# Qkv norms and weight splits moved into the first stage, and the sampled tokens' cross attention rebuilt on 32-column quarters with x's reload beside it

## The reference, cut to what matters

```python
(c_q, c_kv, k_r, z_mla, conv_b, conv_c, conv_h, z_conv, q_x, z_x, gates) = split(h @ w_in)
q     = rms_norm(c_q, q_norm_g) @ w_uq          # heads, then rotary on the last 32 columns
c_kv  = rms_norm(c_kv, kv_norm_g);  k_r = rope(k_r)          # both are outputs as well
y_mla = latent_attention(...)                   # prompt: causal; sampled: 4096 cached positions and the new ones
y_x   = softmax(q_x @ mem_k.T * X_SCALE) @ mem_v             # 4 heads of 128, 256 memory rows
m     = sum over branches of sigmoid(gate) * ((y * silu(z)) @ w_p)
h     = layer_norm(alpha * h + m @ w_o)
```

## Time and profile before

| | us |
|---|---|
| median of 3 runs | 1633.55 |
| lowest, highest | 1630.62, 1635.21 |
| the profiled execution, its own time | 1637.49 |
| its span, first to last instruction | 1635.7 |
| PE busy in the span | 1551.4 (95%) |
| DVE, ACT, POOL busy | 679.7, 443.9, 410.4 |
| mean granted TensorE clock | 0.97 |

### The profile page before, as it was taken

The page is one execution under the profiler, slowest core; times in us unless marked ns, Lnnn a source line. Parts: engine busy times, 40 slices in busy tenths (PEclk is TensorE's granted clock), DMA queues, the critical chain, the costliest instruction groups (busy, mean ns, idle before and its releaser), DMA issues.

```text
span 1635.7 us, 26131 instructions
## 1 busy us (share of the span) xinstructions
PE 1551.4 (95%) x10008; PEld 1365.9 (84%) x10008; DVE 679.7 (42%) x1484; ACT 443.9 (27%) x1067; POOL 410.4 (25%) x295
## 2 busy tenths in 40 slices
PE   7996989999999999969699999999999999999997
PEld 7995967775677777744599999999999999999885
DVE  4204457763533333324334435112644347007744
ACT  4212456661554443411211111111111111113200
POOL 3001046672022222000122222222222222124322
PEclk9997989999999999979599999999999999999999
DMA  5200120002634555223611212111111112112321
GB/s 210 76 1 13 31 78 1 1 1 71 196 92 123 159 157 152 69 73 133 174 39 40 52 39 52 46 39 46 41 45 52 46 39 52 39 50 80 117 94 61
DMA packets 101215, 117.88 MB, mean 72 GB/s; under 512 B 11970, under 2 KB 75266, under 8 KB 101092
## 3 DMA queue, kind: packets, MB, share of 16 engines
q1 hardware_dynamic: 99044, 112.02, 23.3%
q0 software_dynamic: 2048, 4.20, 1.0%
HBM read 109.39 MB, written 6.80 MB: 71 GB/s over the span
## 4 chain that ended last, share of the span: by engine, by line
PE 50%; DMA 1%; issue 1%; DVE 0%; POOL 0%; POOLq 0%; SPq 0%; ACT 0%
PE ps L1762 44%; PE ps L1786 5%; DMA p_xs<-x_prompt 1%; PE ps L1736 1%; DMA p_xs<-x_sample 0%; POOL p_h L1858 0%; POOLq L1646 0%; SPq L1676 0%; DVE p_stats L2022 0%; DVE p_h L2033 0%; DVE p_h L2018 0%; DVE p_h L2031 0%; DVE p_xl L1882 0%; ACT p_xh L1797 0%; PE ps L1773 0%
## 5 line engine op out<-in xcount | busy, mean ns | idle before, releaser
L1762 PE MATMUL ps<-p_xh,p_wh 128*128 128x352 f32 (+1 forms) x1152 | 377.1, 327 | 0.9 <-DVE p_xl L1882 0.9
L1762 PE MATMUL ps<-p_xh,p_wl 128*128 128x352 f32 (+1 forms) x1152 | 376.8, 327 | 0.0
L1762 PE MATMUL ps<-p_xl,p_wh 128*128 128x352 f32 (+1 forms) x1152 | 376.5, 327 | 0.0
L1848 POOL TENSOR_TENSOR p_wl<-p_wr,p_wh 128x512 fp32r<-128x512 f32 x120 | 167.1, 1407 | 665.2 <-DVE p_wh L1871 665.2
L1762 PEld LDWEIGHTS ps<-p_xh,p_wh 128*128 128x128 f32 x1152 | 217.0, 188 | 1.0 <-ACT p_xh L1797 1.0
L1762 PEld LDWEIGHTS ps<-p_xl,p_wh 128*128 128x128 f32 x1152 | 217.6, 189 | 0.0
L1762 PEld LDWEIGHTS ps<-p_xh,p_wl 128*128 128x128 f32 x1152 | 216.7, 188 | 0.0
L1871 DVE CAST p_wh<-p_wr 128x512 fp32r<-128x512 f32 x120 | 46.8, 424 | 346.0 <-ACT p_stage L1833 254.4
L1833 ACT ACTIVATE p_stage<-ps 128x384 f32<-128x384 f32 x168 | 79.4, 473 | 366.1 <-PE ps L1762 366.1
L830 POOL TENSOR_SCALAR p_pr<-p_pr,p_rec 128x896 f32<-128x896 f32 (+3 forms) x64 | 109.6, 1722 | 120.1 <-DVE p_rec L792 120.0
L871 POOL DMA_INDIRECT p_rawr<-cache_kr,p_rows x64 | 64.9, 1013 | 223.6 <-PE ps L1159 162.5
(11 more groups left out here) (286 smaller groups left out, 2755.3 us busy)
## 6 DMA issues: line engine op xcount, KB each, us to landing
p_rawc<-cache_ckv SPq DMA_DIRECT2D x256, 128.0 KB
p_wr<-w_in SPq DMA_DIRECT2D x104, 256.0 KB
p_xs<-x_prompt SPq DMA_DIRECT2D x16, 512.0 KB
p_kv<-cache_mem_k SPq DMA_DIRECT2D x8, 512.0 KB, 10.3
p_kv<-cache_mem_v SPq DMA_DIRECT2D x8, 512.0 KB, 10.7
p_wr<-w_o SPq DMA_DIRECT2D x16, 256.0 KB
p_x<-x_prompt SPq DMA_DIRECT2D x8, 512.0 KB, 3.5
y_p<-p_h SPq DMA_DIRECT2D x8, 512.0 KB, 2.6
```

Of the source, the lines that this page charges most:

```text
L1762: last = pe.matmul(ps[:, g % 8, 0:tn], w[:, v % HL, kt % UK, :], x[:, kt, t0:t0 + tn], start=(kt == 0 and q == 0), stop=(kt == nk - 1 and ...
L1848: nc.gpsimd.tensor_tensor(wl[:, v % HL], wr[:, v % RAW], f32(wh[:, v % HL]), ALU.subtract).then_inc(wl_done, 1)
```

## The change: what it does

- **Qkv's preparation.** The roots, all 9 norms, the split of `w_uq`, `w_uk`, `w_uv`, the rotation of k_r, the casts and the loads of tables and norm weights are moved from `make_qkv` to `project_latents`, behind the last latent tile on each engine's list. The split q_x columns get buffers of their own (`whq`, `wlq`), so that the split `w_uq`, `w_uk`, `w_uv` can lie where the latent columns were. `make_qkv` keeps transposes, splits of the transposed tiles, products and the rotation of q; its output DMAs are issued at its start.
- **Cross attention of sampled tokens.** Each head gets its own 32-column quarter of the PE array (`tile_position=(0, h * 32)`): head h's scores go to PSUM rows 32h to 32h+31 (8 rows used, the others zeros), its values to the same rows and 128 columns. Row-wise work is now on 128 partitions; the probabilities are transposed as 128 x 128, the output with one transpose.
- **x's reload in it.** In step r of the same 12-step pipeline PE also transposes x's tile r (`turn_x`), ACT and DVE split it. Keys and x have one pair of PSUM banks each (before: two). The key and value buffers are 6 (before: 8). SP's list is k, v and x tile by tile, each x load from the third on waiting for `turn_x` of two tiles before; then the convolution's loads and the first 4 weight units, which DVE splits in steps 9 to 11 and POOL finishes. `merge` starts at its matmuls. `clear_sems` stands ahead of `cross_decode`; none is between it and `merge`.

```diff
@@ project_latents, DVE behind the loop over the latent tiles
+            dve.wait_ge(squared, 2 * NT)
+            for j, n in ((0, QL), (1, KVL)):
+                last = dve.tensor_scalar(ms[:, :, j:j + 1], k["ssq"][:, :, j:j + 1], 1.0 / n, EPS, ALU.mult, ALU.add)
+            last.then_inc(mean, 1)
...
+            for i in range(NT):
+                r = rows(i)
+                dve.tensor_scalar(tok[0:r, i, 0:QL], tok[0:r, i, 0:QL], rstd[0:r, i, 0:1], None, ALU.mult)
+                dve.scalar_tensor_tensor(out=tok[0:r, i, QL:QL + KVL], in0=tok[0:r, i, QL:QL + KVL],
...
+            for t in range(QT):
+                dve.wait_ge(uq_step, t + 1)
+                dve.tensor_copy(uqh[:, t, :], uq[:, t, :]).then_inc(w_split, 1)
...
@@ project_latents, SP behind its other loads
+            sp.wait_ge(turned, NT)
+            sp.dma_start(gq[:, :], a["q_norm_g"][0].rearrange("(t p) -> p t", p=P),
...
+            sp.wait_ge(wl_done, NW)
+            sp.dma_start(k["cos"][:, :, :], a["cos"]).then_inc(got, 16)
...
@@ project_latents, ACT ahead of the q_x pieces
+            act.wait_ge(mean, 1)
+            nc.scalar.activation(rt[:, :, :], ms[:, :, :], ACT.Sqrt).then_inc(root, 1)
+            act.wait_ge(lat_done, NT)
+            act.wait_ge(k["uq_in"], 48)
+            for j in range(2):
+                nc.scalar.activation(kvh[:, j], k["ukv"][:, j], ACT.Copy).then_inc(kv_split, 1)
...
@@ make_qkv, PE
             def turn(i):
-                pe.wait_ge(normed, i + 1)
...
@@ cross_decode, SP
+            for b in range(DECB):
+                if b >= KVS:
+                    sp.wait_ge(o_done, b - KVS + 1)
+                for j, (name, kv_in) in enumerate((("cache_mem_k", k_in), ("cache_mem_v", v_in))):
+                    sp.dma_start(kv[:, b % KVS, j], a[name][0, b].rearrange("(t p) h d -> p t (h d)", p=P)
+                                 ).then_inc(kv_in[b], 16)
+                x_dma(b)
+            x_dma(NPT)
...
@@ cross_decode, PE
             def turn(b):
-                if b >= 2:
-                    pe.wait_ge(kt_done, b - 1)
+                if b:
+                    pe.wait_ge(kt_done, b)
...
             def scores(b):
                 for h in range(XH):
-                    last = pe.matmul(ps[0:R, 4, 0:MEM], q[:, b, h, :], kT[:, b % 2, h, :], start=(h == 0),
-                                     stop=(h == XH - 1))
+                    last = pe.matmul(ps[h * R:(h + 1) * R, 4, 0:MEM], q[:, b, h, :], kT[:, b % 2, h, :], start=True,
+                                     stop=True, tile_position=(0, h * R))
...
             def values(b):
                 for j in range(MT):
-                    last = pe.matmul(ps[0:R, 6, :], pt[:, b % 2, j, :], kv[:, b, 1, j, :], start=(j == 0),
-                                     stop=(j == MT - 1))
+                    for h in range(XH):
+                        last = pe.matmul(ps[h * R:(h + 1) * R, 6, 0:XD], pt[:, b % 2, j, h * R:(h + 1) * R],
+                                         kv[:, b % KVS, 1, j, h * XD:(h + 1) * XD], start=(j == 0), stop=(j == MT - 1),
+                                         tile_position=(0, h * R))
...
+            def turn_x(i):
+                pe.wait_ge(x_in[i % 2], 16 * (i // 2 + 1))
+                if i:
+                    pe.wait_ge(xh_done, i)
+                    pe.wait_ge(xl_done, i)
+                for t in range(KT):
+                    last = pe.transpose(ps[:, 2 + t // 4, (t % 4) * P:(t % 4) * P + r],
+                                        xs[0:r, i % 2, t * P:(t + 1) * P], k["ident"][0:r, 0:r])
+                last.then_inc(x_turned, 1)
+            for r in range(DECB + 4):
+                in_step(((r, turn), (r - 1, scores), (r - 2, turn_probs), (r - 3, values), (r - 4, turn_out)))
+                if r < NT:
+                    turn_x(r)
+                elif r == NT:
+                    turn_conv()
@@ cross_decode, ACT
+            for r in range(DECB + 2):
+                in_step(((r - 1, exps), (r - 2, keep_probs)))
+                if r < NT:
+                    x_high(r)
@@ cross_decode, DVE
+            for r in range(DECB + 4):
+                in_step(((r, keys), (r - 1, maxima), (r - 3, normalise), (r - 2, inverse), (r - 4, keep_y)))
+                if r < NT:
+                    x_low(r)
+                else:
+                    v = r - NT
+                    dve.wait_ge(w_got[v], 16)
+                    dve.tensor_copy(wh[:, v], wr[:, v]).then_inc(wh_done, 1)
+            dve.wait_ge(w_got[EARLY - 1], 16)
+            dve.tensor_copy(wh[:, EARLY - 1], wr[:, EARLY - 1]).then_inc(wh_done, 1)
@@ cross_decode, POOL
+            for v in range(EARLY):
+                pool.wait_ge(wh_done, v + 1)
+                nc.gpsimd.tensor_tensor(wl[:, v], wr[:, v], f32(wh[:, v]), ALU.subtract).then_inc(wl_done, 1)
@@ hybrid_step
-        cross_decode(nc, ps, a, k, decode_at)
         clear_sems()
-        merge(nc, ps, a, k, keep.at)
+        shared = merge_space(nc, k, keep.at)
+        cross_decode(nc, ps, a, k, keep.at, shared)
+        merge(nc, ps, a, k, shared)
```

More of the change, by code:

```diff
@@ L396, in _ @@
         def _(act):
-            act.wait_ge(mean, 1)
-            nc.scalar.activation(rt[:, :, :], ms[:, :, :], ACT.Sqrt).then_inc(root, 1)
-            act.wait_ge(k["uq_in"], 48)
-            for j in range(2):
-                nc.scalar.activation(kvh[:, j], kv[:, j], ACT.Copy).then_inc(kv_split, 1)
             def hi(i):
@@ L1416, in _, with merge_jobs @@
                 gather_rotary(nc, a, e, n)
-def cross_decode(nc, ps, a, k, at):
-    m = Map(nc, at)
+def merge_jobs():
+    jobs = []
+    for br, z0 in ((1, C_ZC), (2, C_ZX), (0, C_ZM)):
+        for j in range(4):
+            if br == 1:
+                jobs += [("c", br, j, C_C + j * P), ("h", br, j, C_H + j * P), ("b", br, j, C_B + j * P)]
+            jobs.append(("z", br, j, z0 + j * P))
+        gates = [("gate", br, d, C_G + br * D + d * P) for d in range(KT)]
+        projs = [("proj", br, d, d * P) for d in range(KT)]
+        jobs += gates + projs if br == 0 else [job for pair in zip(gates, projs) for job in pair]
+    return jobs
@@ L1594, in merge, with _ @@
-def merge(nc, ps, a, k, at):
+                if r < NT:
[6 more added lines that the diff above has]
+            dve.tensor_copy(wh[:, EARLY - 1], wr[:, EARLY - 1]).then_inc(wh_done, 1)
+        @block.gpsimd
+        def _(pool):
+            for v in range(EARLY):
+                pool.wait_ge(wh_done, v + 1)
+                nc.gpsimd.tensor_tensor(wl[:, v], wr[:, v], f32(wh[:, v]), ALU.subtract).then_inc(wl_done, 1)
@@ L1597, in merge @@
+def merge(nc, ps, a, k, e):
     jobs = merge_jobs()
-    UK = 4
-    units = [(j, u) for j, job in enumerate(jobs) for u in range(1 if job[0] == "proj" else 2)]
+    units = merge_units(jobs)
     first_unit = [next(v for v, (j, _) in enumerate(units) if j == n) for n in range(len(jobs))]
-    RAW, HL, ST = 4, 6, 8
-    m = Map(nc, at)
-    xh, xl = m("p7_xh", [P, KT, T], F32R), m("p7_xl", [P, KT, T], F32R)
-    mt_at = m.at
-    mt = m("p7_mt", [P, KT, T])
-    u_at = m.at
-    uh, ul = m("p7_uh", [P, 4, T], F32R), m("p7_ul", [P, 4, T], F32R)
@@ L1843, in _ @@
         def _(pool):
-            for v in range(NU):
+            for v in range(EARLY, NU):
                 pool.wait_ge(wh_done, v + 1)
```

385 lines of the change are left out of this document (177 added, 208 removed).

## The result

| | before | after |
|---|---|---|
| median, us (4 runs each, same chip) | 1633.61 | 1586.63 |
| lowest, highest | 1630.62, 1635.21 | 1585.85, 1589.11 |
| the profiled execution, its own time | 1637.49 | 1586.74 |
| its span | 1635.7 | 1584.9 |
| mean granted TensorE clock | 0.97 | 0.984 |

The ratio is 0.9725, with a 95% interval of 0.9707 to 0.9743: 47 us faster. The forecast was 1587.0. The sum inside it was right to some 2 us in each of its large terms, and one loss of 2.5 us that it had not foreseen went against them. The new kernel's four times are 1585.85 to 1589.11 us, so that single executions differ by some 3 us and only the trace can tell terms of that size apart.

The account below looks back on a forecast made before the run. PE's gapless 714.06 us of merge matmuls stays untouched, so gains come ahead of it: 14.5 + 1.3 + 30.8 = 46.6 us, against the median 1633.55 giving 1587.0 us; own range 1581 to 1592 (70%), wider range 1579 to 1603.

Parts of the forecast that it names:

- Qkv's preparation: Start of make_qkv: with preparation moved behind the latents, the first product starts at 136.95 instead of 151.44, gaining 14.5 us.
- The cover: DVE's 47.65 us of idle time behind the latents hides the moved work, put at 28 us, leaving 20.
- rival 5: First stage: moved preparation, ACT's root and casts, holds up the q_x pieces; 15.8 us not won, time 1603; chance 3%.
- The clock: First product step in make_qkv: up to 2.5 us more if the clock does not fall; the middle, 1.3 us, taken.
- The stretch: First load of memory keys to first merge matmul, 726.29 to 811.79: the merge starts at 781.0, gaining 30.8 us.
- the ring of 4.62: New cross attention stage: x_low, keys, maxima, exp, probabilities' copy, x_high and hand-overs on DVE and ACT set each step.
- PE's own work per step: New cross attention stage: transposes, scores and values sum to 3.9 us, under the step's 4.6, so PE waits each step.
- Scores and values: Cross attention on quarters of the PE array: scores take 0.55 us and values 0.9 us per step.
- rival 1: New cross attention stage: quarters do not overlap, PE's step is 6.15 us, +10.9 us, time 1598; chance 10%.
- rival 2: New cross attention stage: clock stays at 1.2 GHz, PE's step 7.3 us, 17 us more, time 1604; chance 9%.
- rival 3: New cross attention stage: loads at 174 GB/s bound the step at 9.0 us, +31 us, time 1618; chance 6%.
- Rival 4: Merge: moved buffers slow the 4320 matmuls, slower than before from 6.5% on; at 8% time 1644; chance 2%.

Follow-up runs that it names:

- the kernel with three small changes: Changed kernel with maxima ahead of key copies, x's halves at a multiple of 64 bytes, two of four weight units split in the stage: 1572.81 us, ratio 0.9667.
- the kernel with maxima first: Changed kernel with DVE taking the maxima of scores(r-1) ahead of its copy of keys(r): 1577.07 us, ratio 0.9702.
- the variants of before: Kernel before with only merge placement moved: `mh` low, `oh` in the middle, 1632.69 us; `mh` low, `oh` high, 1633.38; only `oh`, `ol` high, 1635.26.
- the kernel with the aligned halves: Changed kernel with x's halves starting 32 bytes lower, at a multiple of 64 bytes (159680): 1581.96 us, ratio 0.9741.

## Why the prediction was right

**Qkv's preparation, 14.5 us.** Measured 14.81. From the start of the last q_x copy to the first product it took 3.13 us (133.50 to 136.63) where 3.12 was worked out (133.83 to 136.95); the other 0.3 us are the first stage's, which ended sooner in this execution. The cover that was left, put at 20 us or more, was 27.33. No price of the moved norms reached the path, and rival 5 is out.

**The clock, 1.3 us.** Measured 2.53, the upper end of 0 to 2.5. The rows of before could not have decided it, and even the code does not: the kernel with three small changes has the same first two stages, and there the clock fell in the same window, which this is in that kernel:

```profile
136.00:140.00 4.00, 3.68 (x13) 3.71 (x14) 0.97 (x3) 0.00 (x0) 0.00 (x0) 0.57 0.70 183
```

Its variant with `mt` moved has 0.57 there too, six other kernels with this code have 1.00. In the kernel with three small changes the first step took 7.94 us (136.32 to 144.26) in place of 6.45. So the term differs between executions.

**The stretch, 30.8 us.** Measured 32.94, from three terms counted from the end of y_mla. The first x_low starts after 10.43 us (716.79 - 706.36), predicted 12.41 (738.45 - 726.04): the first three transfers landed sooner than in the row of before, turn_x(0) starting after 7.37 us (713.73 - 706.36) and not 9.36 (735.4 - 726.04). The eight steps took 34.21 (751.00 - 716.79), predicted 35.05: the ring of 4.62 was 4.51. From the last x_low to the first merge matmul 8.17, predicted 7.5: DVE's split of a unit waited behind the last normalise and keep_y, so POOL's four subtractions did not run back to back (a pause of 0.57 us at 754.44 and one of 0.36 at 756.07). 1.98 + 0.84 - 0.67 = 2.15 us. PE's own work per step was put at 3.9; it is 3.74 in the kernel with maxima first, where its pieces have no gaps. The ring was named by its right members in the right order, and moving one of them out shortened the step, so the step is shown and not only fitted.

**Scores and values.** Priced at 0.55 and 0.9 us, measured 0.57 (733.53 to 734.10) and 0.58 (734.46 to 735.04). The first was near; the second was too high: it priced each instruction at 0.055 us by pairs, where four go beside each other and one takes 0.036 (0.58/16). Off the path, it cost the forecast nothing; on one set of columns both are 1.84 us, which rival 1 had right, and its 10.9 us came out as 12.3 in the traces (65.1 against 52.8) and 13.5 in the times: 7 steps by 6.17 - 4.51 = 1.66 are 11.6, the rest lies in the pipeline's first and last steps and between executions.

The Trainium skill's "TensorEngine Tiling (Array Packing)", section Key Properties, warns of a drain at each change of the tiling mode. The mode changes four times in each step here, not six as the prediction counted. The rows neither show a drain nor exclude one. Each of the two quartered pieces takes 0.57 to 0.58 us, 0.11 to 0.12 more than a quarter of its 1.84 on one set. And in the timeline of the kernel with maxima first, the two transposes of the probabilities take 0.27 us (715.52 to 715.79) when x's transposes follow, which have the same shape, and 0.37 (718.92 to 719.29) when the quartered values follow. So up to some 0.1 us may go to a change, which these rows don't separate from the hand-over between pieces. It stayed off the path, as the prediction said it would while PE's sum is under the ring's.

**Rivals 2 and 3.** The clock was 1.00 in every window of 4 us from 720 to 748 and 0.98 in the next, with PE at 2.46 to 3.80 busy of 4.00. (The price of 17 us for rival 2 was short: with 8 transposes at 1.97 twice and the other 1.85 us doubled PE's step is 7.6 and not 7.3, which makes 21 us.) The swinging of the clock that the Trainium skill tells of in "TensorE: Matmul & The Clock Gate", section "A second HAM failure mode: psum-queue depth-cycling", did not appear with PE's gaps of 0.5 us per step. The loads moved 402 to 415 GB/s from 716 to 740, not the 174 of the reload. They and PE were the next limits, at 3.81 and 3.74 us a step, so rival 3 had one of the right resources at the wrong rate.

**Rival 4, placement.** The mechanism exists, at another place and a smaller size. It was priced for the 4320 merge matmuls, whose piece went from 714.06 to 713.34 (over all kernels it is 713.97 to 714.65 us with x's halves low and 712.91 to 715.90 with them high, the two highest in two of the variants of before, each run once); it struck the 384 long matmuls of the output projection, at 2.9% each, 2.5 us in all. The argument against it ("operands lie in different regions already and run at one pace") was made from the merge's rows and said nothing of w_o's halves, which moved too. The pieces of 10.92 and 76.19 us were there to be read; the prediction looked at one of the two users of the moved region.

**The sum.** The measured terms give 14.8 + 2.5 + 32.9 + 0.7 - 2.5 = 48.4 us. The forecast was 46.6, the medians are 47.0 apart, and the two profiled executions 50.75, with the 2.34 us from the stages in between. The terms missed by +0.3, +1.2, +2.1, +0.7 and -2.5, and what is left is the scatter between executions. That the number came out to 0.4 us is therefore luck; that it came out to a few us is not. The forecast took its sum off the median of the runs. Taken off the profiled execution alone, which lay 3.9 us above that median, it would have been 1590.9.

## What to carry to other kernels

When several engines take turns in a pipeline with one buffer pair, add up the ring of the longest list (here x_low, keys, maxima, exp, probabilities, x_high), each by the start-to-start time of a row, and compare it with the work per step of the busiest engine and with bytes over the rate of a saturated window. The largest of the three is the step, and the difference to the second is all that a reordering can win. When an edit moves a buffer, list every later user of that region and of the one it displaced, and look at the pace of each. Prices of two edits in one stage are not to be added: here the same edit was worth 19.8 or 12.3 us, and the other 20.3 or 12.8, as the other was absent or present.

## What the hardware showed beyond that

Four quarters of 32 columns work beside each other: 8 matmuls of 256 columns take 0.57 us against 1.84 on one set, a factor of 3.2, start to start and with the hand-over in it. The values, 16 of 128 columns on quarters against 4 of 512 on one set, take 0.58 and 1.84 us.

The output projection's 512-column matmuls took 395 to 396 ns each with the moving operand in the top region, and 389 to 390 with it at 40704 or 75520 (0.2333 and 0.2267 us start to start). The merge's matmuls of 384 and 352 columns show no such difference. The four kernels with w_o's halves low (before, Qkv's part alone, quarters without the reload, only `mh` low) have 10.91 or 10.92 us for the first 48, the nine with them at the top 11.18 to 11.20, without an exception.

The clock's low spells differ in place and length between executions of the same stage. In the prompt attention, which no kernel here changed, the profiled execution of the changed kernel shows this:

```profile
210.00:214.00 4.00, 4.00 (x17) 3.58 (x17) 2.12 (x5) 1.07 (x4) 2.89 (x3) 0.50 0.00 0
```

and that of the kernel with three small changes, whose code is the same up to there, this:

```profile
210.00:214.00 4.00, 3.78 (x29) 3.08 (x28) 3.57 (x8) 3.38 (x9) 3.06 (x4) 1.00 0.00 0
```

The last score matmul of the prompt attention (one group by line, first and last start) began at 350.2 us in the first and at 345.9 in the second, 4.3 us apart, although the second had lost time to the low clock at 136 and entered the stage no sooner (198.2 and 198.9). In the kernel with the aligned halves, again with the same code there, the clock was 1.00 from 202 to 210, where the changed kernel had 0.50. So a difference of a few us between two profiled executions must be looked for in the changed stages before it is credited to the change.
